# Stick-breaking stage: projection pieces between the heads, feature-major outputs, sums from split operands

## The reference, cut to what matters

```
qkv = (h @ w_qkv).reshape(B, S, 3, SB_HEADS, SB_HEAD_DIM)
z = q @ k.T * scale                      # per head, keys k_pos < q_pos only
log_keep = where(mask, log_sigmoid(-z), 0)
after = reverse_cumsum(log_keep) - log_keep
w = where(mask, exp(log_sigmoid(z) + after), 0)
o = w @ v                                # then all heads together
x = x + o @ w_o
```

## Time and profile before

| | us |
|---|---|
| median of 3 runs | 1188.27 |
| lowest and highest run | 1181.31 and 1189.44 |
| the profiled execution, its own time | 1185.39 |
| the profiled execution, span of its instructions | 1183.6 |
| granted TensorE clock, mean over the span | 0.971 of full speed |
| TensorE busy | 92% of the span |
| VectorE, ScalarE busy | 59%, 48% |
| stick-breaking heads and what hangs on them | 632.6 to 686.0 us from the start of the span |

### The profile page before, as it was taken

The page is one execution under the profiler, slowest core; times in us unless marked ns, Lnnn a source line. Parts: engine busy times, 40 slices in busy tenths (PEclk is TensorE's granted clock), DMA queues, the critical chain, the costliest instruction groups (busy, mean ns, idle before and its releaser), DMA issues. The chain is left out here.

```text
span 1183.6 us, 17327 instructions
## 1 busy us (share of the span) xinstructions
PE 1087.5 (92%) x7300; PEld 973.0 (82%) x7300; DVE 700.4 (59%) x1009; ACT 572.9 (48%) x846; POOL 102.3 (9%) x94
## 2 busy tenths in 40 slices
PE   2699998899978999998998999999998969999997
PEld 2599897798867877887996789899887968998996
DVE  5678774775465665476543445545555885555544
ACT  3355546633554455345335645334435675444344
POOL 0100028260000001122000001000000200000000
PEclk9999999999989999799898999999999989999999
DMA  9766335442336852203454025555553525555551
GB/s 327 227 186 178 107 107 179 142 143 83 107 107 216 286 173 72 72 1 107 143 178 142 1 89 190 184 180 182 192 193 114 172 78 171 182 183 195 188 178 71
DMA packets 118349, 178.43 MB, mean 151 GB/s; under 512 B 5156, under 2 KB 78018, under 8 KB 118272
## 3 DMA queue, kind: packets, MB, share of 16 engines
q1 hardware_dynamic: 116736, 172.40, 45.2%
q0 software_dynamic: 1120, 2.97, 0.8%
q10 hardware_dynamic: 416, 1.97, 0.4%
HBM read 176.27 MB, written 1.05 MB: 150 GB/s over the span
## 5 line engine op out<-in xcount | busy, mean ns | idle before, releaser
L1191 DVE TENSOR_TENSOR sb_w_lo<-sb_raw,sb_w_hi 128x2048 fp32r<-128x2048 f32 (+2 forms) x141 | 320.3, 2272 | 275.9 <-ACT sb_w_hi L605 275.7
L605 ACT ACTIVATE sb_w_hi<-sb_raw 128x2048 fp32r<-128x2048 f32 (+2 forms) x141 | 266.2, 1889 | 200.0 <-PE G L1954 145.0
L1952 PE MATMUL X<-sb_hT_hi,sb_w_hi 128*128 128x256 f32 x1056 | 303.4, 287 | 13.5 <-DVE sb_hT_lo L1516 9.1
L1954 PE MATMUL X<-sb_hT_hi,sb_w_lo 128*128 128x256 f32 x1056 | 300.8, 285 | 0.0
L1953 PE MATMUL X<-sb_hT_lo,sb_w_hi 128*128 128x256 f32 x1056 | 300.7, 285 | 0.0
L1952 PEld LDWEIGHTS X<-sb_hT_hi,sb_w_hi 128*128 128x128 f32 x1056 | 204.5, 194 | 16.7 <-DVE sb_hT_lo L1516 9.8
L1953 PEld LDWEIGHTS X<-sb_hT_lo,sb_w_hi 128*128 128x128 f32 x1056 | 204.6, 194 | 0.8
L1954 PEld LDWEIGHTS X<-sb_hT_hi,sb_w_lo 128*128 128x128 f32 x1056 | 204.5, 194 | 0.0
L1952 PE MATMUL G<-sb_w_hi,sb_hT_hi 128*128 128x512 f32 x256 | 104.5, 408 | 11.7 <-DVE sb_hT_lo L1906 9.5
L1952 PE MATMUL G<-sb_w_hi,sb_uT_hi 128*128 128x512 f32 x256 | 101.4, 396 | 0.0
L1953 PE MATMUL G<-sb_w_lo,sb_uT_hi 128*128 128x512 f32 x256 | 101.2, 395 | 0.0
(11 more groups left out here) (404 smaller groups left out, 1625.8 us busy)
## 6 DMA issues: line engine op xcount, KB each, us to landing
sb_raw<-in_mlp_w SPq DMA_DIRECT2D x64, 1024.0 KB, 5.4
sb_raw<-in_ada_w SPq DMA_DIRECT2D x24, 1024.0 KB, 5.3
sb_raw<-in_a_in_w SPq DMA_DIRECT2D x16, 1024.0 KB, 5.9
sb_raw<-in_b_in_w SPq DMA_DIRECT2D x16, 1024.0 KB, 5.9
sb_raw<-in_sb_w_qkv SPq DMA_DIRECT2D x12, 1024.0 KB, 5.2
sb_raw<-in_rg_w_in SPq DMA_DIRECT2D x8, 1024.0 KB, 5.8
sb_raw<-in_a_out_w SPq DMA_DIRECT2D x4, 1024.0 KB, 5.0
sb_raw<-in_b_out_w SPq DMA_DIRECT2D x4, 1024.0 KB, 5.1
```

The lines of the kernel that those rows point to most:

```text
L605: nc.scalar.activation(w_hi[s][:, 0:nk * w], raw[b % RAW_SLOTS][:, 0:nk * w], ACT.Copy).then_inc(S["w_hi"], 1)
L1191: nc.vector.tensor_tensor(w_lo[s][:, 0:nk * w], raw[b % RAW_SLOTS][:, 0:nk * w], w_hi[s][:, 0:nk * w].bitcast(F32), ALU.subtract).then_inc ...
L1952: dt32(out, lh, rh, start=first, stop=False, skip_group_check=shared)
L1954: return dt32(out, ll, rh, start=False, stop=last, skip_group_check=shared)
```

## The change

The order of weight blocks changes: four q and k blocks first (heads 0 to 7), the first 512 value features, two q and k blocks, the second value features, the last two q and k blocks, the output projection with both first halves ahead. Only the first six blocks of the stage run ahead of the heads. The other six, and the two first halves of the output projection, are cut into 32 pieces of 6 or 12 matmuls and issued between the heads' steps: three pieces in each of heads 0 to 2, two in each of 3 to 12, one in each of 13 to 15. Their splits, their copies out of PSUM and the output's hi and lo parts are placed in the loops of ScalarE and VectorE.

A head's sums are made from `es_hi` and `es_lo`, float32r, with float32r copies of the two constant matrices: four matmuls for two. Two more elementwise steps make the two parts: `z_hi` on ScalarE and `z_low` on VectorE. Scores run one head ahead and share two banks, G[0] and G[1].

A head's output is feature-major: the values of a pair of heads are the stationary operand, the head's weights are moving, with 256 and 128 columns. Half of the rows of each result are used. So the transposes of the stage ("o2"), the copies into `xn` and the round through `hT_hi` and `hT_lo` are gone. `o2_hi` and `o2_low` split each pair of heads straight out of PSUM into `uT_hi` and `uT_lo`.

Elsewhere three semaphores of the first layer's tail (`u0`, `s1`, `v1` and their partners) become one pair counting three per group, and one unused increment at L1446 is gone. The call numbers of `project` drop by two for the later stages, and the removed `log_exp_tables()` stood ahead of the heads.

The diff, cut to its core:

```diff
@@ -39,6 +39,13 @@
...
+SB_FIRST, SB_LATER = (0, 4, 1, 5), (2, 6, 3, 7)
+SB_PIECES = (3, 3, 3, 2, 2, 2, 2, 2, 2, 2, 2, 2, 2, 1, 1, 1)
+SB_SPLITS = (1, 2, 4, 6, 8, 10, 12)
+SB_READ = (2, 3, 9, 10)
@@ -163,12 +170,16 @@
...
-for n in range(8):
+for n in SB_FIRST:
...
-for n in range(2):
-    token_major("sb_v", qkv, slice(2 * D + n * 512, 2 * D + (n + 1) * 512))
-for n in range(2):
-    token_major("sb_o", I["sb_w_o_2"][0], slice(n * 512, (n + 1) * 512))
+token_major("sb_v", qkv, slice(2 * D, 2 * D + 512))
+for n in SB_LATER[0:2]:
+    feature_major("sb_qk2", qkv, n * 256)
+token_major("sb_v2", qkv, slice(2 * D + 512, 3 * D))
+for n in SB_LATER[2:4]:
+    feature_major("sb_qk3", qkv, n * 256)
+for half in range(2):
+    out_half("sb_o", I["sb_w_o_2"][0], half)
@@ -386,6 +397,10 @@
...
+    es_hi = [tsb(f"es_hi{i}", [P, 3, P], F32R) for i in range(2)]
+    es_lo = [tsb(f"es_lo{i}", [P, 3, P], F32R) for i in range(2)]
+    suffix_r = tsb("suffix_r", [P, P], F32R)
+    neg_r = tsb("neg_r", [P, P], F32R)
@@ -415,22 +430,31 @@
...
+HALVES_FIRST = ("a_out", "sb_o")
+OUT_BANK = {"a_out": G, "b_out": G[2:4] + G[0:2], "sb_o": TB + G[2:4], "rg_o": G}
...
+def sb_dst(f):
+    n = (SB_FIRST + SB_LATER)[f]
+    return (qS if n < 4 else kS)[:, 2 * (n % 4):2 * (n % 4) + 2, :], HD ** -0.5 if n < 4 else 1.0
+def o2_chunk(t, k):
+    return t[k // 4][:, k % 4, :]
@@ -439,7 +463,7 @@
...
+        X_BANK = {"kv": TB + G[0:2], "sb": TB + G[2:4], "m0": [X[0], G[0], G[1], TB[0]], "rg": TB + [G[0], G[2]], "m1": TB + G[0:2]}
@@ -1030,34 +1054,69 @@
...
+    for f in range(4):
...
+    def sb_values(b, t):
+        stage = ("sb_v", "sb_v2")[b]
+        if t == 0:
+            act.wait_ge(S["v_tile"], b + 1)
+        else:
+            act.wait_ge(S["w_used"], last_mm[stage] + 1)
+        nc.scalar.activation(vS[:, t, b * 512:(b + 1) * 512], G[2 + t][:, :], ACT.Copy,
+                             scale=r_sb[:, t:t + 1]).then_inc(S["tm_out"], 1)
+    def z_softplus(h):
+        act.wait_ge(S["z_min"], h + 1)
+        ch.link(nc.scalar.activation(es[h % 2][:, :, :], es[h % 2][:, :, :], ACT.Exp))
+        nc.scalar.activation(es[h % 2][:, :, :], es[h % 2][:, :, :], ACT.Ln, bias=one_col).then_inc(S["z_ln"], 1)
+    def z_hi(h):
+        act.wait_ge(S["z_sp"], h + 1)
+        if h >= 2:
+            act.wait_ge(S["z_sum"], h - 1)
+        nc.scalar.activation(es_hi[h % 2][:, :, :], es[h % 2][:, :, :], ACT.Copy).then_inc(S["z_hi"], 1)
+    def sb_weights(h):
+        act.wait_ge(S["z_sum"], h + 1)
+        if h >= 2:
+            act.wait_ge(S["sb_pv"], h - 1)
+        nc.scalar.activation(ws[h % 2][:, :, :], G[h % 2][:, 0:384].rearrange("p (c n) -> p c n", c=3),
+                             ACT.Exp).then_inc(S["w_exp"], 1)
+    def o2_hi(k):
+        act.wait_ge(S["sb_pv"], 2 * k + 2)
+        for half in range(2):
+            hp = slice(half * HD, (half + 1) * HD)
+            ins = nc.scalar.activation(o2_chunk(uT_hi, k)[hp, :], X[k % 2][hp, half * T:(half + 1) * T], ACT.Copy)
+            if half == 0:
...
+        ins.then_inc(S["o2_hi"], 1)
+    split_for(first_mm["sb_v"])
+    ch.mark(nc.scalar.activation(suffix_r[:, :], const("suffix"), ACT.Copy))
+    ch.link(nc.scalar.activation(neg_r[:, :], const("neg_ones"), ACT.Copy))
+    sb_values(0, 0)
+    z_softplus(0)
+    sb_values(0, 1)
+    split_for(first_mm["sb_v"] + 1)
+    for h in range(BH):
+        z_hi(h)
+        if h + 1 < BH:
+            z_softplus(h + 1)
+        sb_weights(h)
+        if h in (5, 7):
+            sb_values(1, (h - 5) // 2)
+        if h in SB_SPLITS:
+            split_for(first_mm["sb_qk2"] + SB_SPLITS.index(h))
+        if h >= 2 and h % 2 == 0:
+            o2_hi(h // 2 - 1)
+    o2_hi(KC - 1)
@@ -1764,49 +1822,69 @@
...
+    def sb_read(f):
+        if f < 4:
+            dve.wait_ge(S["w_used"], first_mm["sb_qk"] + f + 1)
+        else:
+            dve.wait_ge(S["w_used"], first_mm[("sb_qk2", "sb_qk3")[f // 2 - 2]] + f % 2 + 1)
+        bank = X[(19 + f) % 2] if f < 4 else G[2 + f % 2]
+        dst, scale = sb_dst(f)
+        nc.vector.scalar_tensor_tensor(dst, bank[:, :].rearrange("p (c t) -> p c t", c=2), scale,
...
+    for f in range(4):
+        sb_read(f)
...
+            dve.wait_ge(S["z_lo"], h - 1)
+        nc.vector.tensor_scalar(es[h % 2][:, :, :], G[h % 2][:, 0:384].rearrange("p (c n) -> p c n", c=3), 30.0,
...
+        nc.vector.tensor_tensor(es[h % 2][:, :, :], G[h % 2][:, 0:384].rearrange("p (c n) -> p c n", c=3),
...
+    def z_low(h):
+        dve.wait_ge(S["z_hi"], h + 1)
+        nc.vector.tensor_tensor(es_lo[h % 2][:, :, :], es[h % 2][:, :, :], es_hi[h % 2][:, :, :].bitcast(F32),
+                                ALU.subtract).then_inc(S["z_lo"], 1)
+    def o2_low(k):
+        dve.wait_ge(S["o2_hi"], k + 1)
+        for half in range(2):
+            hp = slice(half * HD, (half + 1) * HD)
+            ins = nc.vector.tensor_tensor(o2_chunk(uT_lo, k)[hp, :], X[k % 2][hp, half * T:(half + 1) * T],
+                                          o2_chunk(uT_hi, k)[hp, :].bitcast(F32), ALU.subtract)
+            if half == 0:
+                ch.mark(ins)
+        ins.then_inc(S["o2_lo"], 1)
...
+    split_for(first_mm["sb_v"])
...
+        z_second(h)
...
+        z_low(h)
+        if h in SB_READ:
+            sb_read(4 + SB_READ.index(h))
+        if h == 0:
+            split_for(first_mm["sb_v"] + 1)
+        if h - 1 in SB_SPLITS:
+            split_for(first_mm["sb_qk2"] + SB_SPLITS.index(h - 1))
+        if h >= 3 and h % 2 == 1:
+            o2_low((h - 3) // 2)
+    o2_low(KC - 1)
+    project("sb_o", 12, "m0")
@@ -2590,20 +2668,18 @@
...
+    for f in range(2, 4):
...
+        if h >= 2:
+            pe.wait_ge(S["w_exp"], h - 1)
+        if h % 4 == 0:
+            pe.wait_ge(S["fm_out"], 19 + h // 2 + 2)
...
+        bank = G[h % 2]
@@ -2613,37 +2689,115 @@
...
+        pe.wait_ge(S["z_lo"], h + 1)
+        bank = G[h % 2]
+        for part in (es_hi[h % 2], es_lo[h % 2]):
+            dt32(bank[:, 0:3 * P], suffix_r[:, :], part[:, :, :].rearrange("p c n -> p (c n)"), start=False, stop=True,
+                 skip_group_check=True)
+            ins = dt32(bank[:, P:2 * P], neg_r[:, :], part[:, 2, :], start=False, stop=True, skip_group_check=True)
+        ins.then_inc(S["z_sum"], 1)
+    def sb_pv(h):
+        pe.wait_ge(S["w_exp"], h + 1)
+        if h % 8 == 0:
+            pe.wait_ge(S["tm_out"], 5 + h // 4 + 2)
+        if h % 2 == 0 and h >= 4:
+            pe.wait_ge(S["o2_lo"], h // 2 - 1)
+        bank, w = X[(h // 2) % 2], ws[h % 2]
+        o = (h % 2) * T
+        vs_ = slice(h // 2 * P, (h // 2 + 1) * P)
+        dt32(bank[:, o:o + T], vS[:, 0, vs_], w[:, 0:2, :].rearrange("p c n -> p (c n)"), start=True, stop=True,
...
+        dt32(bank[:, o + P:o + T], vS[:, 1, vs_], w[:, 2, :], start=False, stop=True,
+             skip_group_check=True).then_inc(S["sb_pv"], 1)
+    def first_head():
+        pe.wait_ge(S["mask_in"], 16)
+        z_scores(0)
+    _, hi, lo = take()
+    for half in range(2):
+        if half == 1:
+            first_head()
+            _, hi, lo = take()
+        for m in range(MT):
+            for c in range(4):
+                k = 4 * half + c
+                ins = passes(G[2 + m][:, :], hT(k, m), (hi[:, c, :], lo[:, c, :]), k == 0, k == KC - 1)
+            if (half, m) == (1, 0):
+                ins.then_inc(S["v_tile"], 1)
+        ins.then_inc(S["w_used"], 1)
+    later = []
+    def sb_piece(i):
+        b, p = i // 4, i % 4
+        if p == 0:
+            later.append(take()[1:])
+        hi, lo = later[-1]
+        if b in (0, 1, 4, 5):
+            bank, c, half = G[2 + b % 2], p // 2, p % 2
+            if p == 0:
+                if b < 2:
+                    pe.wait_ge(S["tm_out"], 5 + b + 1)
+                else:
+                    pe.wait_ge(S["tm_out"], 5 + 2 + b % 2 + 1)
+            cs = slice(c * P, (c + 1) * P)
+            for k in range(4 * half, 4 * half + 4):
+                ins = passes(bank[:, c * T:(c + 1) * T], (hi[:, k, cs], lo[:, k, cs]), hT(k), k == 0, k == KC - 1)
+        elif b in (2, 3):
+            m, pair = p // 2, p % 2
+            if b == 2 and pair == 0:
+                pe.wait_ge(S["fm_out"], 19 + 5 + m)
+            for c in (2 * pair, 2 * pair + 1):
+                k = 4 * (b - 2) + c
+                ins = passes(G[2 + m][:, :], hT(k, m), (hi[:, c, :], lo[:, c, :]), k == 0, k == KC - 1)
+            if b == 3 and p == 1:
+                ins.then_inc(S["v_tile"], 1)
+        else:
+            n, m, pair = b - 6, p // 2, p % 2
+            if (n, p) == (0, 0):
+                pe.wait_ge(S["o2_lo"], 4)
+            if (n, p) == (1, 0):
+                pe.wait_ge(S["fm_out"], 27)
+            ms = slice(m * P, (m + 1) * P)
+            for c in (2 * pair, 2 * pair + 1):
+                ins = passes(OUT_BANK["sb_o"][2 * n + m][:, :], (uT_hi[0][:, c, ms], uT_lo[0][:, c, ms]),
+                             (hi[:, c, :], lo[:, c, :]), c == 0, False)
```

(49 more changed lines are left out.)

98 lines of the change are left out of this document (17 added, 81 removed).

## The result

The changed kernel takes **1169.91 us** (median of 4 runs, 1167.18 to 1172.33) against 1187.7 for the kernel before (4 runs, 1181.31 to 1189.44). The ratio is **0.987**, 95% interval 0.983 to 0.992: 10 to 20 us faster. A second set of runs of the same kernel, on another occasion, gave 0.987 again (0.984 to 0.991). The forecast was 1177.5 with a range of 1169 to 1187. The result fell inside, 0.9 us above the low end, and on the far side of the 1% line that I had drawn.

A forecast was written before the change was run, and what follows sets the result against it. TensorE, busy 92% of the span, was taken to bound the kernel. A 10.5 us section gain less 2.0 of end waits gave 8.5 off 1185.39, 1176.9 (1177.8 from the runs' mean); forecast 1177.5, range 1169 to 1187.

The forecast's parts named there:

- the gain is in the holes alone: Heads' section: a head stays about as long (2.55 us before, 2.56 forecast), so only removed holes bring the gain.
- The holes: TensorE at heads' entry (1.57 us), first heads (6.8 lost, partly half clock) and exit: 12.65 us beyond sixteen steady heads.
- The head's own products: Scores 0.97, sums 0.57, values 0.65, borders 0.20, waits 0.07 and 0.10: 2.56 us per head, 41.0 for sixteen.
- borders: Switches between a projection piece and float32 products on TensorE: 0.10 us each, two per new head.
- The sums, 0.57 or 0.44: Four float32r matmuls per head: 0.57 us from profile rows (128 columns at 0.11), 0.44 by the skill's rule.
- The chain with 0.2 us to spare: From scores to VectorE's low part 1.3 us, hidden because TensorE reaches the sums after one piece, 1.47 us.
- The waits, 3.9 us: New TensorE waits: head 2 0.7, last two heads 0.9 and 0.3, last output-projection block 1.0, MLP's turn 1.0.
- The output projection at the old price: Its matmuls were priced at 0.228 us each as before, with 48 left behind the heads.
- the waits are filled: Rival: ScalarE and VectorE run ahead, the 3.9 us of new waits vanish, gain 12.4, about 1173 us; chance 0.22.
- The loop waits in every head: Rival: slower hand-offs or PSUM reads use up the spare 0.2 us; 0.5 us per head, 1186 us; chance 0.15.
- the chain of two banks: Rival: scores wait for head h's exponential in the shared bank; at 1.4 us per head 1199 us; chance 0.04.
- The clock falls in the loop: Rival: a quarter of the new loop's 87 us at half clock loses 11 us, 1188 us; chance 0.04.

The follow-up runs named there:

- The filled kernel: Kernel before, with 15 dependence-free bf16 products ahead of the heads' entry wait and 29 ahead of the first head's sums: 1183.11 us, ratio 0.997.
- The filled kernel with split sums: Kernel before with sums split into two parts, plus 15 filler products ahead of the first scores and 40 ahead of the first sums: 1210.82 us, ratio 1.019.

## Why the prediction was right, and where its sizes were off

The mechanism was right in the main: the holes are gone, the chain is hidden, and the waits come where they were placed. It was wrong in one sentence, that "the gain is in the holes alone". By its steps:

- **The holes (12.65 us before, 3.06 us of waits now).** Right, and worth 9.6 of the section's 11.8 us. Entry, first heads and exit are gone, and the half clock with them. The filled kernel shows the clock's own part, 3.0 us. Of the other 3.8 lost in the first heads 3.01 are the wait, and 0.8 are starts that lie further apart than in the steady heads.
- **The head's own products, 2.56 us.** This is the mis-sized term: measured 2.26 in the steady state, the pieces' borders included. Over all 16 heads it is 2.36, since 593.24 to 683.52 are 90.3 us, less 5.5 for the rest of the value block, 45.2 for 32 pieces (16 of 1.44, 8 of 1.37, 8 of 1.40) and 1.9 of waits, over 16. That gives **3.3 us** more than forecast. "In other words the head's own time does not fall" was wrong. By parts, for the head of above: the sums took 0.53 instead of 0.57 + 0.07, since the two 128-column products cost 0.06 each and not 0.11, and no wait broke the row. The scores took 0.88 instead of 0.97, but the first product of the piece behind them takes 0.21 where the others take 0.12, so the two belong together: with that piece's border (1.51 - 1.44) they are 0.95 instead of 0.97 + 0.10. The other border is 1.48 - 1.44, 0.04 instead of 0.10. The product with the values took 0.74, and it holds the 0.10 ahead of the next scores: its last part takes 0.31, where 128 columns of float32 take 0.22 in the earlier trace rows. So 0.65 + 0.10 was right. What was too dear is the sums (0.11) and the borders (0.18).
- **The sums, 0.57 or 0.44.** The trace has 0.53. The Trainium skill, "TensorE: Matmul & The Clock Gate", "Back-to-back issue gap", would have made them 0.44 by the rule that it gives for a matmul by itself. For the 128-column products that rule was right (0.056 by it, 0.06 here), and for those of 384 columns the starts lie 0.18 and 0.23 apart, not 0.163. My row, a row of nothing but 128-column products, was the wrong neighbour for one behind 384 columns.
- **The chain with 0.2 us to spare.** Right, and in size too: no sums in the middle of the loop wait, and the low part ends 0.20 us ahead of them (647.47 and 647.67). The run with the pieces behind the sums shows what is hidden, about 1.1 us a head.
- **The waits, 3.9 us.** Measured 0.52 (for 0.7), 0.75 and 0.61 (for 0.9 and 0.3), 0.82 (for 1.0), 0.36 (for 1.0): 3.06. **0.8 us** more gain, nearly all at the turn.
- **The output projection at the old price.** Missed: its 96 matmuls read `uT` now, and their starts lie 0.233 us apart instead of 0.228. The half behind the heads took 13.76 us from 683.52 to 697.28, less 1.18 of waits, against 11.84 forecast (48 x 0.228 and 0.9 for the transposes). That is 0.74 more, of which 0.24 are the starts and the rest the borders around the waits and the turn's transposes. The eight pieces at 1.40 instead of 1.37 add 0.24, together about **1.0 us**.

The sum corrected: 8.5 + 3.3 + 0.8 - 1.0 = 11.6, of 11.8 measured. So the range held for the section with room, but for the time only by 0.9 us, and that is in part luck. That the time came out 15 us lower by the ratio and not 12 is inside its interval. The runs of the kernel before spread over 1178.7 to 1193.7. Its profiled one lies 2.3 us under its median, and the profiled one of after 2.2 over its own.

Of the rivals, "the waits are filled" had the nearer time (1173) for the wrong reason: 3.06 of the 3.9 us of waits were there, and the head was cheaper. "The loop waits in every head" and "the chain of two banks" did not happen. The second's wait showed once, with all pieces ahead of the sums. "The clock falls in the loop" got 0.04, and for this kernel it stayed away. But it was the most dangerous of the four: the same sums without pieces, in the kernel before or in the changed one, run the whole loop at 0.50. The heads with pieces were the right neighbours. The Trainium skill, "TensorE: Matmul & The Clock Gate", "A second HAM failure mode: psum-queue depth-cycling", has short idle times between groups of matmuls make the clock go down and up again. The filled kernel with split sums agrees in so far as the clock fell right behind a 1.58 us wait (0.96, then 0.50). It does not agree in that the clock then stayed down under a TensorE that was not idle, and in that the kernel with its pieces behind the sums kept 1.00 through eight heads with a wait of 1.1 us each. Nothing here shows why.

The chances put the mass (0.59) within 1%, with the line at 1176.4 just under a forecast of 1177.5. A term mis-sized by 3.3 us was enough to cross it.

## What to carry to other kernels

Here a chain of small steps over three engines was best covered by independent dense matmuls placed on both sides of its wait, half before and half behind (ratios 0.987, against 0.995 with all before, 1.016 with all behind and 1.033 with none). First ask what covers the chain, and only then lengthen it with an edit that saves TensorE's work: the same split of the sums cost 2% bare and gave about 0.3% covered. Price a matmul by a row with the same columns and the same neighbours. A border moves time between two groups, so add the groups on both sides of it before you call one of them cheaper.

## What the runs showed of the hardware

- A loop of narrow products can run at half clock throughout while TensorE is busy all the time: 66.00 of 72.00 us busy at 0.50 in the kernel with only the split sums. In the earlier trace rows a stretch of 2 us was also busy throughout at 0.50. The loop of before, narrow too and without idle time, had 1.00 once past its first heads:
```profile
656.00:660.00 4.00, 4.00 (x26) 1.00 0.00 0
```
  The two loops differ by four one-pass products in place of two float32 ones and by the longer chain. What decides between them is open.
- Once at half clock such a loop hides its own waits: the chain of 3.43 us fits into the 4.15 us that TensorE then needs, so the trace shows no idle time, and only the granted clock tells.
- Fillers kept the clock when they stood in both waits, and not when they stood in the second alone: it had fallen by then, 2 us behind the 1.40 us wait of the entry, and they ran at half clock themselves (5.4 us for 29). Fillers in the entry wait alone were not tried.
- Float32r matmuls of 512 columns took 0.233 us with `uT` as the stationary source and 0.228 with `hT`. Why is open.
